# Rotary embedding, decays and latent norms inside two input projections, and first weights asked for a stage ahead

## The reference

```python
# mixer one, u = modulated rms_norm(x): [512, 1024]
proj = u @ w_in
c_q, c_kv, k_rope, k_idx, w_idx, qkv_b, gates = split(proj, (384, 256, 32, 32, 8, 2304, 2048))
c_q, c_kv = rms_norm(c_q, g_cq), rms_norm(c_kv, g_ckv)
o_a = dsa_branch(c_q, c_kv, rope(k_rope), rope(k_idx), w_idx, pos, w_uq, w_uk, w_uv, w_iq)
o_b = dilated_branch(qkv_b, pos)       # rope on q and k, 12 heads of 64 each
z = sigmoid(g_a) * (o_a @ w_up_a) + sigmoid(g_b) * (o_b @ w_up_b)
y = z @ w_o
# mixer two
q_lat, kv_lat, k_rope, rq, rk, rv, rg = split(h @ w_in_2, (256, 128, 32, 512, 512, 512, 512))
y_mla = mla_group(rms_norm(q_lat), rms_norm(kv_lat), rope(k_rope), w_uq_2, w_ukv_2)
y_ret = retention_group(rope(rq), rope(rk), rv, rg)    # decays exp(+-log_g * t) in chunks
y = concat(y_mla, y_ret) @ w_out_2
# rope on halves: x1' = x1*cos - x2*sin, x2' = x2*cos + x1*sin
```

## Time and profile before

| | us |
|---|---|
| median of 3 runs (3360.7 to 3369.31) | 3366.93 |
| the profiled execution | 3369.4 |
| its span | 3367.5 |
| TensorE (PE) busy | 2920.7 (87%) |
| VectorE (DVE) busy | 2037.7 (61%) |
| ScalarE (ACT) busy | 1072.9 (32%) |
| GpSimd (POOL) busy | 850.7 (25%) |

### The profile page before, as it was taken

The page is one execution under the profiler, slowest core; times in us unless marked ns, Lnnn a source line. Parts: engine busy times, 40 slices in busy tenths (PEclk is TensorE's granted clock), DMA queues, the critical chain, the costliest instruction groups (busy, mean ns, idle before and its releaser), DMA issues. The chain is left out here.

```text
span 3367.5 us, 37794 instructions
## 1 busy us (share of the span) xinstructions
PE 2920.7 (87%) x14130; PEld 2474.4 (73%) x14130; DVE 2037.7 (61%) x3383; ACT 1072.9 (32%) x1555; POOL 850.7 (25%) x596
## 2 busy tenths in 40 slices
PE   4999988947669879998866969999989999999998
PEld 4788867834557658786754657999878988888776
DVE  6674744263853243233354434989938888898887
ACT  2221223122333142122311432455533333333333
POOL 0000000021001000000010013567656776676321
PEclk9999998969569979999878889999999999999999
DMA  7865712101013233231200012466678888888995
GB/s 256 260 217 161 260 63 74 49 19 32 1 35 88 66 87 98 90 100 58 88 13 16 1 50 103 144 197 198 191 288 314 315 323 300 304 313 303 342 349 219
DMA packets 298413, 537.37 MB, mean 160 GB/s; under 512 B 12584, under 2 KB 193036, under 8 KB 280460
## 3 DMA queue, kind: packets, MB, share of 16 engines
q1 hardware_dynamic: 211696, 375.72, 32.9%
q0 software_dynamic: 36864, 134.23, 11.2%
q10 hardware_dynamic: 49692, 25.28, 2.7%
HBM read 496.39 MB, written 38.80 MB: 159 GB/s over the span
## 5 line engine op out<-in xcount | busy, mean ns | idle before, releaser
L170 PE MATMUL ps<-query_h_hi,expert_u_hi 128*128 128x384 f32 (+1 forms) x1152 | 399.2, 347 | 4.4 <-ACT expert_u_hi L2164 4.4
L170 PE MATMUL ps<-query_h_lo,expert_u_hi 128*128 128x384 f32 (+1 forms) x1152 | 395.2, 343 | 0.0
L1914 POOL TENSOR_TENSOR expert_u_lo<-feat,expert_u_hi 128x1024 fp32r<-128x1024 f32 x144 | 354.4, 2462 | 142.9 <-ACT expert_u_hi L2164 141.4
L170 PE MATMUL ps<-expert_v_hi,expert_w_hi 128*128 128x512 f32 x768 | 306.3, 399 | 34.2 <-DVE expert_w_lo L2070 31.7
L170 PE MATMUL ps<-expert_v_hi,expert_w_lo 128*128 128x512 f32 x768 | 303.0, 394 | 0.0
L170 PE MATMUL ps<-expert_v_lo,expert_w_hi 128*128 128x512 f32 x768 | 302.5, 394 | 0.0
L170 PE MATMUL ps<-ffn_h_hi,ffn_w_hi 128*128 128x512 f32 x704 | 278.2, 395 | 19.0 <-PEq L556 17.9
L170 PE MATMUL ps<-ffn_h_hi,ffn_w_lo 128*128 128x512 f32 x704 | 275.8, 392 | 0.0
L170 PE MATMUL ps<-ffn_h_lo,ffn_w_hi 128*128 128x512 f32 x704 | 275.6, 391 | 0.0
L217 DVE TENSOR_TENSOR ffn_w_lo<-ffn_w_raw,ffn_w_hi 128x2048 fp32r<-128x2048 f32 x66 | 151.1, 2290 | 162.7 <-ACT ffn_w_hi L213 162.7
L2075 DVE TENSOR_TENSOR expert_v_lo<-peer_s,expert_v_hi 128x1024 fp32r<-128x1024 f32 x128 | 193.6, 1513 | 84.0 <-ACT expert_v_hi L2172 83.7
(11 more groups left out here) (434 smaller groups left out, 6169.2 us busy)
## 6 DMA issues: line engine op xcount, KB each, us to landing
feat<-in_expert_u_blocks SPq DMA_DIRECT2D x64, 1024.0 KB
peer_s<-in_expert_v_blocks SPq DMA_DIRECT2D x64, 1024.0 KB
gate_rows<-expert_gates SPq DMA_DIRECT2D x32, 768.0 KB
ffn_w_raw<-in_w_gate SPq DMA_DIRECT2D x44, 512.0 KB, 4.0
ffn_w_raw<-in_w_up SPq DMA_DIRECT2D x44, 512.0 KB, 5.2
ffn_w_raw<-in_w_down SPq DMA_DIRECT2D x22, 1024.0 KB, 4.8
gate_rows<-in_w_mod SPq DMA_DIRECT2D x18, 1024.0 KB, 5.4
in_w_raw<-in_w_in SPq DMA_DIRECT2D x16, 1024.0 KB, 5.2
```

Source lines behind the costliest of these rows:

```text
L170: return nc.tensor.matmul(out, lhsT, rhs, start=start, stop=stop, skip_group_check=True)
L1914: nc.gpsimd.tensor_tensor(u_lo[:, n % 2, :, :], u_raw[:, n // 2 % 2, n % 2, :, :], u_hi[:, n % 2, :, :], ALU.subtract).then_inc(u_lo_done, 1)
```

## The change

- `stage_project_split` takes lists of rotations (`ropes`, with decays), norms and the job after which the norms may run. VectorE does all six operations of a rotation itself, two token tiles per slot, for a job whose copies are done; ScalarE takes squares and roots at slot 2 * norms_after + 3, VectorE scales at the slot after. Stages nr1 and nr3 are gone; nr2 and nr4 keep their rotations (`stage_rope`).
- The order of jobs: in mixer one the three q and k jobs come first, then both latents, then v; in mixer two rq, rk, latents, rv, rg.
- The bias is loaded by SP within the turn's stage, and VectorE waits for it at the start of the attention.
- The first two weight slots of uq1 and uq2 are asked for in the turn before (`ProjectWeights`).
- The 14 pieces of the gated split are done inside the gated stage; its first slot is asked for after 4 low parts, its second after 8.
- The first two slots of o1 are loaded, rounded and split at the end of the gated stage, those of o2 in the y split. One weight stream serves both, with its slots counted on (`ws.before`).

```diff
-def stage_split(nc, b, tag, jobs):
+def stage_split(nc, b, tag, jobs, ws, next_jobs):
...
+        @block.sync
+        def _(sp):
+            for m in range(2):
+                job_slot(ws, sp, next_jobs, m)
...
+            for m in range(2):
+                job_round(ws, act, next_jobs, m)
...
+class ProjectWeights:
...
+    def load_first(self, sp):
+        for n in range(2):
+            self.load(sp, n)
...
-    ws.load(sp, m, m % 2, [(0, HALF, src[:, (m % 2) * HALF:(m % 2 + 1) * HALF, :])], m < 2)
+    ws.load(sp, ws.before + m, m % 2, [(0, HALF, src[:, (m % 2) * HALF:(m % 2 + 1) * HALF, :])], ws.before + m < 2)
...
+        def rope(dve, q):
+            n, x1, x2, cos, sin, decay = ropes[q]
...
+            dve.wait_ge(out_act, 2 * (n + 1))
+            dve.wait_ge(out_dve, 2 * (n + 1))
+            nc.vector.tensor_tensor(tmp(0), x1, cos, ALU.mult)
+            nc.vector.tensor_tensor(tmp(1), x2, sin, ALU.mult)
+            nc.vector.tensor_tensor(tmp(2), x2, cos, ALU.mult)
+            nc.vector.tensor_tensor(tmp(3), x1, sin, ALU.mult).then_inc(multiplied, 1)
+            dve.wait_ge(multiplied, q + 1)
+            nc.vector.tensor_tensor(x1, tmp(0), tmp(1), ALU.subtract)
+            nc.vector.tensor_tensor(x2, tmp(2), tmp(3), ALU.add).then_inc(rotated, 1)
+            if decay:
+                dve.wait_ge(rotated, q + 1)
+                nc.vector.tensor_tensor(decay[0], decay[0], decay[1], ALU.mult)
...
+                    if norms and m == 2 * norms_after + 3:
+                        norm_roots(act)
...
                 for m in range(n_slots + 2):
                     if first <= m < n_slots:
-                        ws.rest(dve, m, m % 2, HALF * width[m // 2])
+                        job_rest(ws, dve, jobs, m)
                     if m >= 2 and m % 2 == 0:
                         if add_row is None:
                             evacuate(dve, m // 2 - 1, (1, 3), nc.vector.tensor_copy, out_dve)
...
+                    for _ in range(2):
+                        if q < len(ropes) and ropes[q][0] <= m // 2 - 1:
+                            rope(dve, q)
+                            q += 1
+                    if norms and m == 2 * norms_after + 4:
+                        norm_scale(dve)
...
@@ stage_gated_up
+                    if m == 0:
+                        sp.wait_ge(split_lo, DC // 2)
...
+                    if m == 0:
+                        sp.wait_ge(split_lo, DC)
...
+                for m in range(2):
+                    job_slot(ws, sp, next_jobs, m)
...
+                    else:
+                        job_round(ws, act, next_jobs, 0)
                     act.wait_ge(z_sum, m + 1)
                     nc.scalar.activation(z[0][:, m, :], part[:, j, 0, :], ACT.Copy).then_inc(z_hi_done, 1)
+                job_round(ws, act, next_jobs, 1)
...
+                    else:
+                        job_rest(ws, dve, next_jobs, 0)
                     dve.wait_ge(sig_done, m + 1)
...
+                job_rest(ws, dve, next_jobs, 1)
...
@@ mixer_one
-                with nc.Block() as block:
-                    @block.sync
-                    def _(sp):
-                        sp.dma_start(bias[:, :, :], d["dilated_bias"].rearrange("p (r n) -> p r n", r=TT)).then_inc(bias_in, 16)
-                        sp.wait_ge(bias_in, 16)
+
+                def load_bias(sp):
+                    sp.dma_start(bias[:, :, :], d["dilated_bias"].rearrange("p (r n) -> p r n", r=TT)).then_inc(bias_in, 16)
```

More of the change, by code:

```diff
@@ L907, in _ @@
             def _(sp):
[L908 to L913, removed]
+                for n in range(slots, len(jobs)):
+                    sp.wait_ge(up, (n - slots + 1) * TT)
+                    weights.load(sp, n)
             @block.tensor
@@ L979, in stage_project_split @@
         out_dve = b.sem(f"{tag}_out_dve")
+        stat = own.enter_context(nc.sbuf_tensor(f"{tag}_stat", [P, max(1, len(norms)), TT], F32))
+        multiplied = b.sem(f"{tag}_multiplied")
+        rotated = b.sem(f"{tag}_rotated")
+        squares = b.sem(f"{tag}_squares")
+        rooted = b.sem(f"{tag}_rooted")
+        inverted = b.sem(f"{tag}_inverted")
         n_slots = 2 * len(jobs)
@@ L1067, in stage_turn, with _ @@
     with nc.Block() as block:
+        if prefetch:
+            @block.sync
+            def _(sp):
+                prefetch(sp)
         @block.tensor
@@ L1096, in _, with stage_rope @@
                     ins.then_inc(out_dve, 1)
-def stage_norm_rope(nc, b, tag, norms, ropes, copies=(), decays=()):
+def stage_rope(nc, b, tag, ropes, copies):
     with ExitStack() as own:
@@ L1489, in stage_gated_up @@
     with ExitStack() as own:
-        ws = WeightStream(nc, b, own, "gated", b.feat_slots)
+        chunks = [(src[:, k, :], hi[:, k, :], lo[:, k, :]) for src, hi, lo in parts for k in range(src.shape[1])]
+        split_hi = b.sem("gated_split_hi")
+        split_lo = b.sem("gated_split_lo")
         sig = b.tok[:, 0:2, :].rearrange("p j (g n) -> p j g n", g=2)
@@ L2421, in rope_items, with job_ropes, shared_ropes @@
     return out
+def job_ropes(b, n, t, c0, heads, pos, decay=None):
+    out = []
+    for i in range(TT):
+        v = cols3(t, i, c0, heads, DH)
+        half = DH // 2
+        cos = b.cos[:, pos * TT + i, ROPE_A // 2:ROPE_A // 2 + half].unsqueeze(1).to_broadcast([P, heads, half])
+        sin = b.sin[:, pos * TT + i, ROPE_A // 2:ROPE_A // 2 + half].unsqueeze(1).to_broadcast([P, heads, half])
+        factors = decay and (v, b.const(decay)[:, i * HEADS:(i + 1) * HEADS].unsqueeze(2).to_broadcast([P, HEADS, DH]))
+        out.append((n, v[:, :, 0:half], v[:, :, half:DH], cos, sin, factors))
+    return out
+def shared_ropes(b, n, t, c0, pos):
+    half = ROPE_A // 2
+    at = slice(pos * TT, (pos + 1) * TT)
+    return [(n, t[:, :, c0:c0 + half], t[:, :, c0 + half:c0 + 2 * half], b.cos[:, at, 0:half], b.sin[:, at, 0:half], None)]
 def mixer_one(nc, b, d):
@@ L2559, in mixer_one @@
         z = b.split_pair(mix, "z", DC)
+        ws = WeightStream(nc, b, mix, "gated", b.feat_slots)
+        ws.before, ws.dmas_before, ws.first = 2 * DC, 32 * DC, True
+        jobs = output_jobs(b, d["w_o"].rearrange("a k n -> (a k) n"), z)
         with ExitStack() as gated:
```

165 lines of the change are left out of this document (96 added, 69 removed).

## The result

| | before | changed |
|---|---|---|
| median of four runs each, taken together | 3363.81 us | 3277.29 us |
| lowest to highest | 3358.84 to 3369.31 | 3260.95 to 3290.94 |
| the profiled execution, its span | 3369.4, 3367.5 | 3272.07, 3270.3 |
| TensorE clock granted, mean of the span | 0.925 | 0.936 |

The changed kernel takes 0.9738 of the time (95% interval 0.97 to 0.9776): 86.5 us less. 3267 was forecast, with 3250 to 3288 around it. The forecast of the time held, and one of its rivals came true in part as well.

What follows compares the result with a forecast made beforehand. TensorE sets the pace, so time is won only where it idles: 42.4 + 30.7 + 4.2 - 0.8 + 9.4 + 6.2 + 5.3 + 3.0 = 100.4 us off, giving 3267 us, range 3250 to 3288 (own case 3255 to 3280).

Steps and rivals of the forecast that it cites:

- The two holes: TensorE's idle gaps before the dilated and retention turns shrink to 1.0 and 1.1 us, winning 42.4 and 30.7 us.
- such a start: At uq1, a stage start at half clock over some 3.4 us costs half of that, 1.7 us.
- VectorE's slots: In the projections, VectorE's rotations at 0.41 us per product fit between weight splits; TensorE never waits, no table load counted.
- The rival that priced the product at 0.94: In the projections VectorE becomes the bound, 38 us lost, total 3305 us; chance 0.05.
- both slacks: In the projections, low halves are ready 3.1 us, or 1.9 with decays, before TensorE wants them at 10.88.
- The clock after the holes: Both turns keep the clock: 6.0 us instead of 7.8 and 4.2 instead of 6.6, 4.2 us won, bounds 0 and 8.
- The early loads: First weights asked for a stage ahead: 6.9 us won at uq1 and uq2, 6.2 at gated, 5.3 at o1, 3.0 at o2.
- the picture at o1: Before o1, slot 0's low half goes ahead of VectorE's products; the chain behind ends 1.1 us later, 5.3 us won net.
- the attention's clock: Rival: clock falls otherwise in unedited attention; 11 us more won in MLA (3256) or 14 lost in dilated (3281); chance 0.14.

Runs made afterwards that it cites:

- e3: Changed kernel with the four products of every rotation done three times: 3295.08 us, ratio 0.9785 to the original.
- e6: Changed kernel with one product and the sum of each rotation moved from VectorE to GpSimd: 3273.1 us, ratio 0.9723 to the original.
- e1: Changed kernel with rotations, norms and decays put back in stages of their own (nr1, nr3), bias load and early weights kept: 3339.32 us, ratio 0.9919 to the original.
- e5: Changed kernel with the attention bias loaded in a stage of its own again, ahead of the dilated turn: 3276.7 us, ratio 0.9723 to the original.
- e2: Changed kernel with first weights asked for as each stage begins and the gated split a stage of its own: 3291.85 us, ratio 0.9769 to the original.
- e11: Changed kernel with only o1's slot 0 low half taken after the gated stage's last two products instead of before: one run, 3281.08 us.
- e4: Changed kernel run again with nothing edited: 3269.36 us over six runs, ratio 0.9704 to the original.
- e7: Changed kernel with one 512-column matmul into an unread bank per item 12 to 24 of the DSA attention: 3269.48 us, ratio 0.9712 to the original.
- e8: Changed kernel with unread matmuls ahead of gated, o1 and o2, and o1's slot 0 low half after the last products: 3266.66 us, ratio 0.9703 to the original.
- e9: Changed kernel with unread matmuls in the DSA attention and ahead of gated, o1 and o2, order at o1 unchanged: 3261.98 us, ratio 0.9685 to the original.
- e10: e9 with five more unread matmuls in each norm stage and one per item 2 to 9 of the MLA attention: 3245.95 us, ratio 0.9636 to the original.

## Why the prediction was right

**The two holes** (42.4 and 30.7) were right to 0.1 us as gaps: 43.42 became 0.92, 31.78 became 1.05. In block two 1.1 us of it was given back at the start of in2. There the half rate lasted 5.7 us in the changed kernel (the pace of a matmul goes from 0.43 to 0.23 us at 1568.3, start 1562.61) and 3.3 in the original (1619.1, start 1615.84). That length differs from trace to trace: at the starts of in1, in2, gated, o1 and o2 it is 3.3 to 4.4 us in the original and 3.4 to 6 in the changed kernel. The 3.4 us by which I priced such a start at 1.7 had no row beside it, and it is the low end of that.

**VectorE's slots.** Products 0.42 (0.41 forecast), slack 3.2 us by e3 and 3.3 in the changed kernel's own trace (3.1 forecast), no wait of TensorE for a low half, no table load of ScalarE from 527 to 672 us, where the two roots stand. The rival that priced the product at 0.94 fell because nothing runs on GpSimd; e6 shows that the collision is real and that in projection one the slack covers even it.

What I missed is the narrowest slot. I set both slacks against a slot of 10.88 us, but in block two the last rotations of rk stand in a slot of the 416 wide latents, which lasts 9.0 us (1609.01 to 1618.03). VectorE, then TensorE in order of time, changed kernel: the low half for the next slot, and the matmul that needs it.

```profile
1615.74 1.89 DVE L218 TENSOR_TENSOR in_w_lo<-in_w_raw,in_w_hi 128x1664 fp32r<-128x1664 f32 x1
...
1618.03 0.35 PE L170 MATMUL ps<-in_w_hi,in_h_hi 128*128 128x416 f32 x1
```

It ends at 1617.63, 0.4 us ahead; in the 512 wide slot of the same block the slack is 1.9, as forecast. So nothing was lost, but the margin of the design was 0.4 us and not 1.9, and e6 used it up.

**The clock after the holes** (4.2) came as 3.8; e1 and e5 show it returning with a pause of 37 and of 7.7 us. At uq1 the clock brought 2.4 where I took 1.7, at uq2 nothing where I took 0.8: right as a sum (2.4 for 2.5), wrong one by one. Of the turns I had the gain right and the levels 0.5 us too low: 6.49 and 4.73 us where I wrote 6.0 and 4.2.

**The early loads.** 6.9, 6.3 and 5.0 came where 6.9, 6.2 and 5.3 were forecast. o2 came as 3.7, not 3.0. e2 confirms the sum: 22.5 us for 23.9. What I got wrong in detail is the picture at o1: I held the low half ahead of the products to be a loss. The gap fell by 5.8, and e11 shows that the other order is 1.0 worse. From the gated stage to o1 only 5.0 of the 5.8 are left, for the gated stage's half rate start lasted longer in that trace, 5.7 us for 4.4.

**The step that was off: the attention's clock.** I gave 0.14 to the case that it falls otherwise, and sought it in the dilated and the MLA attention. In the profiled run it came in the DSA attention, a stage that I had not looked at, and took 7.6 us, offset by 5.5 in the peer part. Neither was in the sum; both lie outside the edited code, and that they nearly cancel in this execution is luck. In e4 they stand at 99.56 and 1341.1 us, near the original's 99.66 and 1340.1, and nothing had to cancel. The mechanism was as the rival had it: nothing is edited there, the same loop has either level. Its sizes were off: it priced the MLA attention's slow stretch at 11 us, and the short form saves 8.1. The MLA attention takes one of two values in every trace, whatever the kernel: 68.53, 68.56, 68.58, 68.53, 68.52 and 68.56 us (original, changed, e2, e4, e7, e11), or 60.45, 60.38, 60.47, 60.42, 60.37 and 60.38 (e1, e3, e5, e6, e8, e9), and 60.75 with fillers (e10). In the short ones the clock doesn't fall. Busy time by stretch, second and third 9 us of the stage, changed kernel:

```profile
1786.00:1795.00 9.00, 8.20 (x41) 6.39 (x40) 4.12 (x25) 6.20 (x28) 0.00 (x0) 0.75 0.00 0
1795.00:1804.00 9.00, 9.00 (x35) 7.66 (x34) 2.72 (x14) 3.98 (x14) 0.00 (x0) 0.50 0.00 1
```

and e3:

```profile
1810.00:1819.00 9.00, 7.57 (x49) 5.70 (x47) 4.63 (x28) 6.81 (x31) 0.00 (x0) 1.00 0.00 1
1819.00:1828.00 9.00, 7.76 (x49) 5.75 (x48) 4.54 (x22) 6.19 (x23) 0.00 (x0) 1.00 0.01 2
```

So 8.1 us hang on whether the clock falls. It fell in six of the twelve traces without fillers there, so an honest chance for "one attention differs by 7 or more from the profile" would have been nearer a half than 0.14; the range covered it. What decides between the two values no run shows.

**What stays open.** Why the changed kernel spreads over 33 us and the original over 16 to 19. The clock goes with it (its longer runs have the lower mean), but no kernel was traced at both ends of its spread. e7 and e10 spread over 5.7 and 3.5 us; that fillers narrow it isn't shown, for e2 and e3, which have none, spread over 7.4 and 5.3 us in four runs each, and e9 with them over 9.4 in five. Nor is it shown where the peer part's 1334.6 to 1345.8 us (all traces) comes from.

## What to carry to other kernels

Where one engine sets the pace at full clock, count the others' free time slot by slot and put whole stages of theirs into it; check the longest piece that may stand before what the pacing engine waits for, and check it against the shortest slot in which it can stand, not only the sum. After that, read the granted clock at each stage's first matmuls and through each stage paced by another engine: matmuls into an unread bank (14268 instructions of TensorE in e10 for 14130) bought 23 us here, a quarter of what all the edits together bought. Before VectorE work is moved out of a chain's way, look what GpSimd does in the place it is moved to.

## What the runs showed that I had not expected

- TensorE can be busy without a gap (10.00 of 10 us, twice in a row) and stay at 0.50: for some 19 us in the DSA attention of the changed kernel's trace, in which e4, the same code, has 0.88 in the first 10. A pause is not needed for a low clock.
- A GpSimd sum of 1.26 us takes 3.25 if a VectorE subtraction of 2.29 us starts 0.16 us before it (e8), and 3.24 in e11.
- At half rate a matmul of 416 columns paces at 0.35 us and one of 512 at 0.43; at full rate 0.19 and 0.23.
- The length of a half rate start is not fixed: at the same place, o1, it was 3.4 us in the changed kernel's first trace and 5.6 in e4, the same code.
- Fillers also moved the whole distribution, not only its best case: the slowest run of e10 (3248.74) is 9 us faster than the fastest of ten of the changed kernel (3257.83).
